# Two address offsets in a two-block layer stack: the norm's operand 64 bytes off the weights' alignment, the last of four weight slots 96 bytes further on

## The reference

```python
# block 1, layer i: retention and gated delta mixers, then a dense FFN (i = 0) or 8 experts, top 2 (i = 1)
h = mixer_block(h, norm_mix[i], w_in[i], ...)          # u = rmsnorm(h, g); proj = u @ w_in; ...; h + merged @ w_out
u = rmsnorm(h, norm_ffn[i])
h = h + (swiglu(u, ...) if i % 2 == 0 else moe(u, ...))
h = h + sigmoid(rmsnorm(h, norm_ple[i]) @ w_ple_gate[i]) * (p[i] @ w_ple[i])
# block 2, layer l: mLSTM, differential attention and HGRN mixers, then an FFN of width 4096
u = rmsnorm(x, norm1_g[l]) @ w_in_2[l]; ...; x = x + mix @ w_out_2[l]
x = x + square(relu(rmsnorm(x, norm2_g[l]) @ w_up[l])) @ w_down[l]
```

## Time and profile before

| | us |
|---|---|
| median of 3 runs | 2193.05 |
| lowest and highest | 2187.59, 2194.86 |
| the profiled execution | 2192.61 |
| its span, first to last instruction | 2190.8 |
| TensorE matmul busy | 2121.4 (97%) |
| TensorE weight load busy | 1977.7 (90%) |
| DVE busy, ACT busy | 1530.3 (70%), 1367.5 (62%) |
| DMA engines, mean share | 54.5% |

### The profile page before, as it was taken

How to read it: one execution, slowest core, us unless ns; L and a number is a source line. 1 busy time by engine, 2 the same in 40 slices (tenths; PEclk the granted TensorE clock), 3 DMA queues, 4 the chain that set the end, 5 groups by cost and what they waited for, 6 DMA issues and landing times.

```text
span 2190.8 us, 37308 instructions
## 1 busy us (share of the span) xinstructions
PE 2121.4 (97%) x15466; PEld 1977.7 (90%) x15466; DVE 1530.3 (70%) x2189; ACT 1367.5 (62%) x1884; POOL 65.5 (3%) x102
## 2 busy tenths in 40 slices
PE   8999999999999999997999999999989999999999
PEld 7988999999989889997888888888879999978999
DVE  5777456665567774563889999976858665875664
ACT  6765575544567655754877777776765545775553
POOL 0003000000000030000000000000000000000000
PEclk9999999999999999997999999999999999999999
DMA  7434345656554343452999999954415665423553
GB/s 265 148 118 124 97 140 183 192 160 193 168 167 151 117 124 95 142 188 105 334 330 336 325 324 329 341 206 145 142 39 174 192 191 161 161 71 118 196 187 135
DMA packets 126449, 400.68 MB, mean 183 GB/s; under 512 B 26048, under 2 KB 26432, under 8 KB 126272
## 3 DMA queue, kind: packets, MB, share of 16 engines
q1 hardware_dynamic: 126272, 398.20, 54.1%
HBM read 395.79 MB, written 2.36 MB: 182 GB/s over the span
## 4 chain that ended last, share of the span: by engine, by line
PE 83%; ACT 6%; DVE 6%; POOL 2%; issue 2%; DMA 0%; SPq 0%; DVEq 0%; ACTq 0%; POOLq 0%
PE ps L466 82%; DVE wlo L2117 2%; ACT scr L1374 1%; ACT whi L1364 1%; ACT arena L1374 1%; DVE arena L2117 1%; DVE arena L2125 1%; POOL arena L3068 1%; DVE scr L2117 1%; POOL arena L3071 1%; ACT L1374 1%; ACT L1368 0%; ACT rst L1374 0%; PE ps L1050 0%; DVE h L2117 0%
## 5 line engine op out<-in xcount | busy, mean ns | idle before, releaser
L2117 DVE TENSOR_TENSOR wlo<-raw,whi 128x1024 fp32r<-128x1024 f32 (+2 forms) x622 | 747.0, 1214 | 301.9 <-ACT whi L1364 296.1
L1364 ACT ACTIVATE whi<-raw 128x1024 fp32r<-128x1024 f32 (+2 forms) x622 | 643.8, 1043 | 318.2 <-PE ps L466 314.0
L466 PE MATMUL ps<-uh,whi 128*128 128x256 f32 x2240 | 648.8, 290 | 11.5 <-DVE arena L2125 3.9
L466 PE MATMUL ps<-uh,wlo 128*128 128x256 f32 x2240 | 629.3, 281 | 0.0
L466 PE MATMUL ps<-ul,whi 128*128 128x256 f32 x2240 | 629.1, 281 | 0.0
L466 PE MATMUL ps<-arena_r,whi 128*128 128x256 f32 x2720 | 479.3, 281 | 7.1 <-DVE arena_r L2117 6.2
L466 PEld LDWEIGHTS ps<-uh,whi 128*128 128x128 f32 x2240 | 421.7, 188 | 24.4 <-issue 13.3
L466 PEld LDWEIGHTS ps<-ul,whi 128*128 128x128 f32 x2240 | 422.4, 189 | 5.7 <-issue 5.3
L466 PEld LDWEIGHTS ps<-arena_r,whi 128*128 128x128 f32 x2720 | 417.2, 190 | 11.3 <-issue 7.8
L466 PEld LDWEIGHTS ps<-uh,wlo 128*128 128x128 f32 x2240 | 421.9, 188 | 0.0
L466 PE MATMUL ps<-arena_r,wlo 128*128 128x256 f32 x1360 | 379.4, 279 | 0.0
(11 more groups left out here) (175 smaller groups left out, 2244.9 us busy)
## 6 DMA issues: line engine op xcount, KB each, us to landing
raw<-stream SPq DMA_DIRECT2D x586, 512.0 KB, 4.1
arena<-stream SPq DMA_DIRECT2D x64, 512.0 KB, 5.7
CO<-stream SPq DMA_DIRECT2D x44, 512.0 KB, 5.5
raw<-stream SPq DMA_DIRECT2D x32, 384.0 KB, 4.7
arena<-stream SPq DMA_DIRECT2D x20, 384.0 KB, 4.6
CO<-stream SPq DMA_DIRECT2D x12, 384.0 KB, 4.5
CO<-const SPq DMA_DIRECT2D x2, 704.5 KB, 6.8
h<-xT SPq DMA_DIRECT2D x4, 256.0 KB, 5.9
```

The lines of the kernel that those rows point to most:

```text
L466: return self.e.matmul(o, l, r, start=start, stop=stop, skip_group_check=True)
L1364: self.e.activation(M.whi[:, b:b + n], M.raw[a][:, 0:n], ACT.Copy).then_inc(K.sem("weight_hi"), 1)
L2117: return self.e.tensor_tensor(o, a, b, op)
```

## The change

`apart` and `STEP` go. `uh` and `ul` become dense, 8 tiles of 256 elements without gaps, and the whole of each begins `OFF` = 16 elements (64 bytes) into its tensor. `M.UG[0]` and `M.HT` lose their gaps (`UG[0]` had none) and move 64 bytes up within the arena. The last of the four slots of `whi` and of `wlo` begins `SHY` = 24 elements (96 bytes) further on than densely packed; the tensors grow by 32 elements each. The number, order and waits of all instructions are the same on all engines; some instructions of ACT and DVE that wrote two or four tiles with a gap between write one run.

Bytes past a multiple of 128 of the built program:

| operand | before | after |
|---|---|---|
| `whi`, `wlo`, slots 0 to 2 | 32 | 32 |
| `whi`, `wlo`, slot 3 | 32 | 0 |
| `uh`, `ul` (`M.U`) | 32, 64, 96, 0, ... by tile | 96 |
| arena operands of `proj_T` and `down` | 96 | 96 |
| `M.UG[0]` | 96 | 32 |
| `M.HT` | 96, 0, 32, 64, ... by tile | 32 |

`wlo` and `ul` also come to lie 128 bytes further on past a multiple of 256 than before.

```diff
-STEP = 8
+OFF = 16
+SHY = 24
...
-def apart(ap, n):
-
-    return v3(ap, n + STEP)[:, :, 0:n]
...
-        self.whi, self.wlo = sb("whi", NSPLIT * CH, F32R), sb("wlo", NSPLIT * CH, F32R)
-        self.h = sb("h", 2048)
-        self.hT, self.U = v3(self.h), tuple(apart(sb(x, 2048 + 8 * STEP, F32R), T) for x in ("uh", "ul"))
+        self.whi, self.wlo = (self.split_slots(sb(x, NSPLIT * CH + 32, F32R)) for x in ("whi", "wlo"))
+        self.h, uh, ul = sb("h", 2048), sb("uh", 2048 + 2 * OFF, F32R), sb("ul", 2048 + 2 * OFF, F32R)
+        self.hT, self.U = v3(self.h), tuple(v3(x[:, OFF:2048 + OFF]) for x in (uh, ul))
...
-        self.UG = [[v3(ARr[:, 4096 + i * 2048:6144 + i * 2048]) for i in range(2)], self.U]
-        n = 11 * (P + STEP)
-        self.HT = [apart(ARr[:, 8192 + i * n:8192 + (i + 1) * n], P) for i in range(2)]
+        at = 4096 + OFF
+        self.UG = [[v3(ARr[:, at + i * 2048:at + (i + 1) * 2048]) for i in range(2)], self.U]
+        at = 8192 + OFF
+        self.HT = [v3(ARr[:, at + i * 1408:at + (i + 1) * 1408], P) for i in range(2)]
...
+    def split_slots(self, ap):
+
+        return [ap[:, i * CH + SHY * (i == NSPLIT - 1):(i + 1) * CH + SHY * (i == NSPLIT - 1)] for i in range(NSPLIT)]
...
-        at = self.split % NSPLIT * CH
-        self.split += 1
-        return i, (v3(self.M.whi[:, at:at + n], ncol), v3(self.M.wlo[:, at:at + n], ncol))
+        j, self.split = self.split % NSPLIT, self.split + 1
+        return i, (v3(self.M.whi[j][:, 0:n], ncol), v3(self.M.wlo[j][:, 0:n], ncol))
```

More of the change, by code:

```diff
@@ L1362, in rounded @@
                 self.wait_ge(*K.when("used", K.split_at[j - NSPLIT]))
-            a, b = K.raw[i][0], j % NSPLIT * CH
-            self.e.activation(M.whi[:, b:b + n], M.raw[a][:, 0:n], ACT.Copy).then_inc(K.sem("weight_hi"), 1)
+            a, b = K.raw[i][0], j % NSPLIT
+            self.e.activation(M.whi[b][:, 0:n], M.raw[a][:, 0:n], ACT.Copy).then_inc(K.sem("weight_hi"), 1)
     def ln_exp(self):
@@ L2110, in rounded @@
             j, self.split = self.split, self.split + 1
-            a, b = K.raw[i][0], j % NSPLIT * CH
+            a, b = K.raw[i][0], j % NSPLIT
             self.wait_ge(K.sem("weight_hi"), j + 1)
-            self.tt(M.wlo[:, b:b + n], M.raw[a][:, 0:n], M.whi[:, b:b + n].bitcast(F32), SUB).then_inc(
+            self.tt(M.wlo[b][:, 0:n], M.raw[a][:, 0:n], M.whi[b][:, 0:n].bitcast(F32), SUB).then_inc(
                 K.sem("weight_lo"), 1)
```

## The result

The changed kernel takes 2199.54 us (median of 7 runs, 2196.59 to 2200.66) against 2193.05 us (7 runs, 2187.59 to 2195.17): 1.0033 times the time before, 95% interval 1.0023 to 1.0042. It is slower by 0.33%, at the edge of what a measurement of this kernel tells from no change. The forecast was 2177 us, 0.7% faster.

The account below looks back on a forecast made before the run. TensorE, busy 97% of the span, was taken as the bound, through its matmul pace. Terms of -21.8, +3.9 and -1.5 us gave -19.4, less 17% given back -16.1, hence 2177 us; range 2160 to 2201.

Parts of the forecast that it names:

- The bound: Whole kernel: TensorE, busy 97% of the span, sets the time; the change acts only through the pace of matmuls.
- 622 pieces of the prediction: Weight pieces going round four slots, from which 5040 of the 6720 `M.U` matmuls were put in slots 0 to 2.
- Addresses as a cause: Narrow matmuls: pace depends on streamed start less next loaded start modulo 128; 113.3 or 117.8 ns at 64, 118.3 rotating.
- rival B: Narrow matmuls: distance isn't the cause, `M.U` stays at 118.3 ns, slot 3 is neutral; 2193 us, chance 0.12.
- The term of `M.U`: `M.U` streams in slots 0 to 2: 5040 matmuls gain 4.33 ns each at fixed distance 64, -21.8 us.
- The fast share of slots 0 to 2: Streams in weight slots 0 to 2: share running at 113.3 rather than 117.8 ns, put at 0.85.
- rival C: Half: state out of slot 3 a toss, or distance counts modulo 256; fast share 0.5, 2187 us, chance 0.15.
- The arena's term: Arena streams: 1020 matmuls in slot 3 lose +3.9 us, 3060 in slots 0 to 2 gain -1.5 us.
- Slot 3's own price: Slot 3 at fixed distance 96: taken as 118.3 ns per matmul, between bounds of 113.3 and 120.0.
- The experts' 0: Experts' wide matmuls loading `UG[0]` or `HT`, moved to distance 0: no change, bounds -5.2 and +5.2 us.
- The 17% given back: Whole chain: DVE, ACT, POOL and issue hold 17%, so that share of TensorE's -19.4 us turns into waits, leaving -16.1.
- A: The slow pace wins: streams leave slot 3 slow, slots 0 to 2 at 117.8 ns; +16, 2209 us, chance 0.18.

Follow-up runs that it names:

- e6: Kernel before with `uh` and `ul` dense and not moved, so distance 0 for `M.U`: 2207.2 us, ratio 1.0058.
- e7: Kernel before with `uh` and `ul` dense and 96 bytes further on, so distance 96 for `M.U`: 2211.2 us, ratio 1.0091.
- e1: Kernel before with only `uh` and `ul` made dense and begun 64 bytes further on, places modulo 256 kept: ratio 1.0017.
- e2: Changed kernel with slot 3 of `whi` and `wlo` packed densely, `wlo` and `ul` still moved by 128 bytes: 2185.3 us, ratio 0.9981 to before.
- e5: Kernel before with `uh` and `ul` dense at +64 and `ul` alone 128 bytes further on modulo 256: 2198.5 us, ratio 1.0028.
- e4: Kernel before with `uh` and `ul` dense at +64 and `wlo` alone 128 bytes further on modulo 256: ratio 0.9965.
- e11: Changed kernel with `ul` alone back at its old place modulo 256, slot 3 still shifted: ratio 1.0012 to before.
- e3: Kernel before with only slot 3 of `whi` and `wlo` begun 96 bytes further on: 2196.4 us, ratio 1.0026.
- e8: Kernel before with `uh` and `ul` dense at +64, but their eighth tile at 0 modulo 256: 2199.5 us, ratio 1.0031.
- e9: Kernel before with only `UG[0]` and `HT` dense and 64 bytes further on, as in the changed kernel: ratio 1.0001.
- e12: Kernel before with `UG[0]` and `HT` moved as in the change and `wlo` 128 bytes further on, `M.U` keeping its gaps: ratio 0.9991.
- e13: Changed kernel with `ul` at its old place and, instead of slot 3's shift, gaps inside slot 3 that rotate the distance: 2181.26 us, ratio 0.9952 to before.
- e14: Changed kernel with `ul` and `wlo` at old places modulo 256 and gaps inside slot 3 instead of its shift: 2201.6 us, ratio 1.0047 to before.

## Why the prediction was wrong

**The bound held.** TensorE's pace was nearly the whole of it: 6.2 of the 7.4 us; counts, the largest waits and the busy times of DVE and ACT stayed. The 622 pieces of the prediction are one group of the earlier trace rows; with those read from other buffers there are 762 in the trace, which changes no term, since the counts of matmuls were read directly.

**Addresses as a cause held, and rival B fell.** With `M.U` dense and the weights in place, distances of 0 and 96 cost 120.0 ns (e6, e7), 64 has paces of 113.3 and 117.8 (e1). The granted clock was 1.00 in all these stretches. Equal shapes at equal clock differ by 6% with the addresses alone. The rule of the Trainium skill cited there ("TensorE: Matmul & The Clock Gate", section "Step-by-step: what each phase is for": loading weights takes no read bandwidth from the running matmul) has no room for that; here the measurement decides.

That the difference modulo 128 is what counts is not shown, and it isn't the whole: a distance of 96 costs 120.0 ns in e7 and 118.2 to 118.4 in slot 3 of the changed kernel, where the places modulo 256 are others. No run moved both operands by the same amount, which would tell a difference from a place.

**The term of `M.U`, -21.8 us, failed; it measured -2.6.** The fast share of slots 0 to 2, put at 0.85, was 0 for `M.U` and 0.43 for the arena. Two steps of the term were wrong. First, the case was equated with the arena's by the distance modulo 128. The change also moved `ul` by 128 bytes, which I had listed and put no more than a chance on (rival C). With `ul` there the fast pace doesn't occur: none of some 200 pieces in slots 0 to 2, in the changed kernel, in e2 and with `ul` alone moved (e5), against 0.42 of them with `wlo` alone (e4). Second, even with every place modulo 256 kept (e1) only 7% of the pieces are fast. A stream at distance 64 seldom starts fast by itself there; the rotating `M.U` that I counted as lost time was what started the arena's streams fast, and the change took it away.

**The arena's term, +3.9 - 1.5 us, was mis-sized and in part of the wrong kind; it measured +11.1.** Slot 3's own price was right, and partly by luck: 118.3 was taken over from the rotating stream, 118.4 is the mean, but a fixed 96 at other places costs 120.0 (e7). But "a stream that comes out of slot 3 is fast, whatever it was" is false: with `wlo` moved it flips (after, e11), with `wlo` in place it keeps what it had (e3). The row on which the step stood showed a rotation that ended on distance 96, and I took the end for the cause. With that end alone no stream behind it was fast (e8), nor with a fixed 96 throughout (e7); the rotation does it (before, e9, e12), and in e13 one inside slot 3, with `wlo` moved.

**The experts' 0** was within its bounds: -2.3 us, to which distance 0 adds only together with `wlo`'s move (e9 against e12).

**The 17% given back** can't be judged in the changed kernel, where there was no gain to give back; no run was made for it, and it stays open.

**The rivals.** What happened is nearest to C, whose two mechanisms both occurred in a form: slot 3 changes the pace (an exchange, not a toss) and the place modulo 256 of `wlo` and `ul`. But it was priced with half of `M.U`'s pieces fast, where none were, and so came out at 2187. A, the only case on the slower side, had the right end (2209, or from 2199 on where some streams are fast) by the wrong mechanism: the slow pace won for `M.U` because the fast one wasn't to be had. That the measured 2199.5 us lies below 2201, the upper end of the range, owes nothing to the forecast's mechanism.

What stays open: the change with both `wlo` and `ul` at their old places modulo 256 was not run; e1 and e3, which hold its two main parts that way, are each slower than before. Open too is why these places give two paces, and what draws one at a start. Only paces and orders are in the trace, and start addresses in the program; nothing in them shows how the two reads meet. A rotation of `M.U` starts arena streams fast with either place of `wlo` (ten of ten before, eight in e12), while one inside slot 3 does it only with `wlo` moved (e13, e14); the first rotates the streamed operand, the second the loaded one in the other direction, and these were not tried apart.

## What to carry to other kernels

Where TensorE streams without pauses, read the pace from the distances between starts, per buffer slot, before counting instructions: here 24 matmuls in a piece took 2.72, 2.83 or 2.88 us with nothing else different but addresses and history. A pace that depends on what ran before must be varied on the chip in the sequence in which it will run, and a layout change of one operand has to be costed for the streams behind it too. Keep all relative addresses of an untouched part (here modulo 256) when testing the offset of another: 128 bytes of padding decided which paces could occur at all, and putting `ul` alone back took the changed kernel from 1.0033 to 1.0012 of the time before (e11).

## What the runs showed of the hardware that was not expected

A stream of 256-column matmuls on weights loaded one ahead has two paces at one and the same set of addresses, 113.3 and 117.8 ns (118.9 with `wlo` 128 bytes further on), and keeps the one it has for over 500 matmuls (before, from 524.8 us on). A passage of 24 matmuls in the shifted slot exchanges them when `wlo` is at 160 modulo 256 (29 of 33 passages of arena operands after) and not when it is at 32 (1 of 33 in e3). And the best place differs by role: with activations streamed, distance 0 is the slowest beside 96 (120.0 ns, e6 and e7); with the same activations loaded and 512 weight columns streamed it is the fastest that was run (228.0 ns in e6 against 232.6 before).
